# First block's inverse by levels: the product xx of levels 1 to 5 gives way to transposes of XT and a ScalarE copy, in a weave of five more steps a head with 0.94 instead of 1.12 dense steps a round

## The reference

```
decay = jnp.exp(jnp.where(causal, G[..., :, None] - G[..., None, :], -jnp.inf))
kk = jnp.einsum('bhnik,bhnjk->bhnij', k, k)
lmat = jnp.where(strict, beta[..., :, None] * kk * decay, 0.0)
amat = jnp.eye(CHUNK, dtype=q.dtype) + lmat
rhs = jnp.concatenate([v * beta[..., None], k * (beta * jnp.exp(G))[..., None]], -1)
sol = lax.linalg.triangular_solve(amat, rhs, left_side=True, lower=True, unit_diagonal=True)
```

## Time and profile before

| | |
|---|---|
| median of 3 runs | 2263.67 us (2260.33, 2263.67, 2264.84) |
| span of the profiled execution, first to last instruction | 2261.5 us |
| TensorE busy, share of the span | 2066.9 us, 91% |
| DVE, ACT, POOL busy | 42%, 28%, 20% |
| the woven heads and dense tiles | about 116 to 716 us of the span |

### The profile page before, as it was taken

How to read it: one execution, slowest core, us unless ns; L and a number is a source line. 1 busy time by engine, 2 the same in 40 slices (tenths; PEclk the granted TensorE clock), 3 DMA queues, 4 the chain that set the end, 5 groups by cost and what they waited for, 6 DMA issues and landing times.

```text
span 2261.5 us, 24322 instructions
## 1 busy us (share of the span) xinstructions
PE 2066.9 (91%) x10160; PEld 1516.4 (67%) x10160; DVE 943.3 (42%) x1370; ACT 643.6 (28%) x966; POOL 451.9 (20%) x310
## 2 busy tenths in 40 slices
PE   7999999999999979888788879898888899999999
PEld 5878888888887763333333337677655677888787
DVE  7865445433333662111011025865643894222333
ACT  4533422322323311000000024353134763222231
POOL 5432132231322511111111011321001220000021
PEclk9999999999999979998899889999998999999999
DMA  5751421221324369999999964202111133332210
GB/s 168 255 141 47 93 57 38 38 75 45 68 38 152 140 230 397 409 405 406 408 414 406 420 270 169 100 13 72 47 47 37 47 121 122 102 112 75 95 73 38
DMA packets 97657, 361.28 MB, mean 160 GB/s; under 512 B 9850, under 2 KB 34588, under 8 KB 85256
## 3 DMA queue, kind: packets, MB, share of 16 engines
q1 hardware_dynamic: 86800, 335.34, 41.4%
q0 software_dynamic: 8240, 19.00, 2.5%
q10 hardware_dynamic: 2504, 5.35, 0.8%
HBM read 338.94 MB, written 29.10 MB: 163 GB/s over the span
## 4 chain that ended last, share of the span: by engine, by line
PE 81%; DVE 8%; issue 5%; ACT 4%; POOL 1%; DMA 0%; PEld 0%; PEldq 0%; SPq 0%; ACTq 0%; DVEq 0%; POOLq 0%
PE ps L269 77%; PE ps L273 4%; ACT ST L265 1%; DVE H L259 1%; ACT L265 1%; DVE ST L253 1%; DVE BG L253 1%; ACT M L265 1%; DVE sm L2930 0%; DVE WL L253 0%; DVE ML L253 0%; POOL WL L253 0%; ACT M L266 0%; DVE H L256 0%; DVE BG L259 0%
## 5 line engine op out<-in xcount | busy, mean ns | idle before, releaser
L269 PE MATMUL ps<-W,BG 128*64 128x512 f32 x672 | 202.1, 644 | 31.9 <-issue 31.9
L269 PE MATMUL ps<-XH,WS 128*128 128x512 f32 x704 | 218.6, 392 | 0.0
L269 PE MATMUL ps<-HTH,WL 128*128 128x512 f32 x448 | 180.9, 404 | 0.0
L269 PEld LDWEIGHTS ps<-ST 128*128 128x128 f32 x1376 | 167.5, 192 | 8.6 <-POOL ST L253 1.7
L269 PE MATMUL ps<-ST 128*128 128x64 f32 (+1 forms) x1376 | 167.8, 273 | 1.2 <-POOL ST L253 1.0
L269 PEld LDWEIGHTS ps<-XH,WS 128*128 128x128 f32 x704 | 133.4, 189 | 27.8
L2100 DVE COPY BG<-ps 128x512 f32<-128x512 f32 x32 | 22.1, 692 | 293.0 <-PE ps L269 293.0
L269 PEld LDWEIGHTS ps<-W,BG 128*64 128x64 f32 x672 | 62.1, 148 | 120.0 <-issue 118.5
L269 PE MATMUL ps<-XL,WS 128*128 128x512 f32 x352 | 138.1, 392 | 1.8 <-DVE XL L253 1.8
L269 PE MATMUL ps<-M,BG 128*64 128x512 f32 (+1 forms) x336 | 122.7, 552 | 15.7 <-issue 8.4
L263 ACT ACTIVATE BG<-ps 128x512 f32<-128x512 f32 x48 | 28.5, 595 | 377.8 <-PE ps L273 344.2
(11 more groups left out here) (384 smaller groups left out, 4343.2 us busy)
## 6 DMA issues: line engine op xcount, KB each, us to landing
W<-in_w SPq DMA_DIRECT2D x42, 2048.0 KB, 26.3
W<-in_w_in SPq DMA_DIRECT2D x27, 2048.0 KB, 10.3
ST<-in_w SPq DMA_DIRECT2D x14, 2048.0 KB, 25.4
U<-in_w SPq DMA_DIRECT2D x14, 2048.0 KB, 28.0
M<-in_w SPq DMA_DIRECT2D x13, 2048.0 KB, 28.3
HT<-in_w SPq DMA_DIRECT2D x13, 2048.0 KB, 27.9
W<-in_w_ffn_in SPq DMA_DIRECT2D x22, 1024.0 KB, 7.6
ypad<-BG SPq DMA_DIRECT2D x23, 512.0 KB, 15.1
```

The source lines that it names most:

```text
L269: return p.e.matmul(o, lhsT=l, rhs=r, start=start, stop=stop, skip_group_check=True)
```

## The change

At levels 1 to 5, `xx` is no longer the product of `XT` and `Y`. When DVE has updated `XT`, TensorE transposes all of it (`p_turn4`), and ACT copies from the transpose the half of the columns that the next level's `y` reads. `X` after `x0` is likewise copied only in that half. DVE loses the subtraction of `xx`. A level now has three steps, `y`, `xt` and `xx`, so that a head has 33 rounds and the four pairs 132; the rate becomes 0.94. `VB`, which lies in `X`, now waits for the `y` of level 6.

```diff
@@ p_head
             for n in range(1, 7):
                 p.wait_ge(lc_done[h % 2], 6 * (h // 2) + n)
-                if 1 < n < 7:
+                if n > 1:
                     p.wait_ge(*B["xx", h, n - 1].free())
                 p_half(("y", h, n), b0, C, firsts(X, n))
                 yield
                 p.wait_ge(*B["y", h, n].free())
-                if n > 1:
-                    p.wait_ge(*B["xt", h, n - 1].free())
+                p_half(("xt", h, n), b0 + 2, Y, seconds(XT, n))
+                yield
                 if n < 6:
-                    p_half(("xx", h, n), b0 + 1, XT, firsts(Y, n))
-                p_half(("xt", h, n), b0 + 2, Y, seconds(XT, n))
-                yield
+                    p.wait_ge(*B["xt", h, n].free())
+                    p_turn4(("xx", h, n), b0 + 1, XT)
+                    yield
@@ v_head
-                if n < 6:
-                    t = B["xx", h, n]
-                    v.wait_ge(*t.full())
-                    if n == 1:
-                        v.wait_ge(*B["x0", h].free())
-                    else:
-                        v.wait_ge(*B["xx", h, n - 1].free())
-                    tt(v, firsts(X, n), firsts(X, n), packed(t, n), SUB).then_inc(t.drained)
...
-            v.wait_ge(*B["xx", h, 5].free())
+            v.wait_ge(*B["y", h, 6].full())
             tt(v, VB, four(t.at), col4(beta[:, :, h]), MUL).then_inc(t.drained)
@@ s_head
-            act(X, four(t.at), ACT.Copy).then_inc(t.drained)
+            act(firsts(X, 1), firsts(four(t.at), 1), ACT.Copy).then_inc(t.drained)
...
                 act(firsts(Y, n), packed(t, n), ACT.Copy).then_inc(t.drained)
                 yield
                 yield
+                if n < 6:
+                    t = B["xx", h, n]
+                    s.wait_ge(*t.full())
+                    act(firsts(X, n + 1), firsts(four(t.at), n + 1), ACT.Copy).then_inc(t.drained)
+                    yield
@@ heads
-            weave([lambda h=h: one(h) for h in range(8)], 2, back, 1.12)
+            weave([lambda h=h: one(h) for h in range(8)], 2, back, 0.94)
```

## The result

| | before | after |
|---|---|---|
| median of the runs | 2262.03 us (4 runs, 2260.33 to 2264.84) | 2301.93 us (4 runs, 2297.65 to 2307.04) |
| span of the profiled execution | 2261.5 us | 2295.4 us |
| woven stage, first `rb,cst` matmul to first matmul of the merging products | 116.56 to 717.12, 600.56 us | 115.89 to 750.73, 634.84 us |
| TensorE idle in it | 16.0 us | 44.8 us |

What follows compares the result with a forecast made beforehand. TensorE's own instructions were taken to set the woven stage's pace. Terms -19.0 + 1.2 + 3.0 + 0.6 + 0.4 - 0.7 + 0.9 = -13.6 us took the span from 2261.5 to 2247.9, median about 2250; range 2243 to 2258.

Steps and rivals of the forecast that it cites:

- The wait of 0.72 us for POOL's mask at level 2: TensorE's wait for GpSimd's mask in the woven stage was to vanish under a third leg of cover: -0.7 us.
- The longer chain within a level: Three legs per level instead of two; waits at the turns only in two or three levels of the first pair: +0.4 us.
- the one on the third leg: Rival: ACT or DVE come late at the turns in most levels; 0.5 us each leaves 2260 us; chance 0.09.
- The price of transposes: The transposes replacing the product in each level: 104 ns each, 0.84 us for a pair's eight.
- the changes between head and dense steps: TensorE's switches in the woven stage: 119 instead of 106, at 0.09 us each, +1.2 us.
- The bare rounds: Eight rounds without dense work: round 1 costs +3.0 us, rounds 17 and 50 together +0.6, the others 0.
- The turns' leg: Worst leg, xt to turn in the convolution's rounds: TensorE waits 0 to 0.2 us; the rival put 0.5 or 0.7.
- columns set the price: Rival: a transpose costs twice a 64-column instruction, so xx saves 0 instead of 19 us: 2267; chance 0.03.
- The clock: Round 1's new wait may lower TensorE's clock afterwards, losing 0 or 1.7 us; half was put in: +0.9 us.
- the prediction's own signs of being wrong: Turn waits for ST over 5 us, stage clock under 0.97 by over 0.01, or experts' weights arriving when before.
- the clock does not hold through the transposes: Rival: each of twenty turns in the levels drops the clock, 1.7 us each, 34 us added: 2284; chance 0.05.
- The end: After the woven stage, the experts' stage: what the woven stage gains or loses is passed to the end nearly whole.

Runs made afterwards that it cites:

- e1: The changed kernel with GpSimd making the masks of levels 2 to 6 two steps earlier, nothing else changed: 2259.53 us, ratio 0.9994.
- e3: The changed kernel with xx again a TensorE product with DVE's subtraction, in its own step ahead of xt, masks left late: 2310.95 us, ratio 1.0224.
- e5: The changed kernel with xx again a product in its own step, as in e3, and masks two steps early, as in e1: 2282.99 us, ratio 1.0092.
- e4: The changed kernel with a rate of 1.0 instead of 0.94: 2285.44 us, ratio 1.0104.
- e11: The changed kernel, masks where they were, with the count of due dense work starting at 0.07: 2297.88 us, ratio 1.0168.
- e9: e1 with the level-1 mask one step earlier too and the count of due dense work starting at 0.07: 2260.02 us, ratio 0.9997.
- e10: e9 with the last sums of squares one step later and in the other PSUM bank: 2258.70 us, ratio 0.9985.
- e12: The changed kernel, masks where they were, with DVE doing all weight and activation splits of the woven stage: 2255.68 us, ratio 0.9983.

## Why the prediction was wrong

**The step that failed** is "The wait of 0.72 us for POOL's mask at level 2 has a third leg of cover now and goes: -0.7 us". That wait was read as a lone one, and a longer level as more cover. The cover that counts is TensorE's work between the dense tile's end, which releases ACT's and GpSimd's splits, and the next `y`. It doesn't grow with the number of legs: the removed product was nearly half of it. The very wait that was to go, at level 2 of the first pair, became the 3.38 us at 166.25. Beside it stands the same fault in "The longer chain within a level": it followed ACT and DVE, the engines whose work changes, and left out GpSimd, which got only an empty step. The rows were to be had: 5.4 us from tile end to mask, 6.3 us of cover, and 6.3 - 2.7 = 3.6 us left after the change (3.8 in the row above). In place of -0.7 stand +20.8 us of mask waits and 2.3 more named "issue". No rival named GpSimd's queue either; the one on the third leg spoke of ACT and DVE, and against it of a single wait for a mask, where the trace has two (0.72 and 0.25 us).

The change of 34.3 us in the stage, by the runs (rounding leaves 0.1):

| part | us | from |
|---|---|---|
| product to transposes and the longer weave | -15.8 | work, e1 less before |
| mask waits | +20.8 | 21.8 less 1.0 |
| other waits, the 2.3 of the level-1 mask among them | +8.0 | idle +28.8, less the line above |
| work lost with the mask waits | +21.2 | work, after less e1 |

The last line is the clock's, as far as the traces tell: e1 and the change have the same instructions in the stage. Summed over stretches of 4 us, the granted clock puts 97 us of the stage at the lower level in the change and 54 in e1; half of the difference, 22 us, is an estimate of the work lost by it.

- **The price of transposes** was right. Eight start to the next matmul in 0.79 us, 99 ns each, where 0.84 was taken:

```profile
363.15 1.03 PE L273 MATMUL ps<-cst,ST 128*128 128x128 f32 x8
...
363.94 0.48 PE L269 MATMUL ps<-HTL,WHM 128*128 128x512 f32 x1
```

- With the changes between head and dense steps -19.0 + 1.2 = -17.8 was forecast; the work fell by 15.8 from before to e1, the clock's share in it (0.97 to 0.96) included.
- **The bare rounds.** Round 1's wait came out at 3.29 us (3.36 forecast), that behind the turns at 0.27 (0.3):

```profile
121.23 2.04 PE L269 MATMUL ps<-ST,BG 128*128 128x128 f32 x8 [3.29 <-issue]
...
377.14 1.97 PE L269 MATMUL ps<-ST 128*128 128x64 f32 x16 [0.27 <-ACT ST L263]
```

- **The turns' leg** (`xt`, subtraction, turn) never waited in the changed kernel; this rival fell. The rival "columns set the price" fell with the 99 ns. Its 2267 was a span; the median would be 2269.
- **Waits not foreseen.** The dense tile behind the small sums waits 4.04 us for ACT, where the copy of a `y`, two splits of 1.05 us and a table load now stand ahead of the square root of 0.27:

```profile
229.50 0.38 ACT L263 ACTIVATE ST<-ps 128x256 f32<-128x256 f32 x1 [1.25 <-PE ps L269]
229.78 1.05 ACT L263 ACTIVATE WHM<-W 128x1024 fp32r<-128x1024 f32 x1
230.72 1.05 ACT L263 ACTIVATE WV<-W 128x1024 fp32r<-128x1024 f32 x1
...
231.78 1.28 ACT L265 ACT_TABLE_LOAD   x1
...
233.08 0.27 ACT L265 ACTIVATE sm<-ps,cst 128x16 f32<-128x16 f32 x1
...
233.50 0.77 PE L269 MATMUL ps<-HTL,WHM 128*128 128x512 f32 x1 [4.04 <-ACT sm L265]
```

  The new copies are not the cause: e3 and e5, which have none of them, wait the same 4.04 us, and e4 doesn't. It is the places that the weave of 0.94 gives to the steps.
- **The clock** had the right mechanism, a fall behind a wait, and half the price of one fall (0.9 us). The runs show 21.2 us of work beside 21.8 us of mask waits. Of the prediction's own signs of being wrong this one came: 0.92 where 0.96 was the limit. The rival "the clock does not hold through the transposes" came nearest in sign and fell in mechanism. From 360 to 380 us, with turns in it, the clock was 1.00:

```profile
360.00:380.00 20.00, 19.72 (x125) 17.18 (x124) 8.15 (x14) 6.09 (x13) 4.63 (x3) 1.00 0.14 35
```

  The Trainium skill ("TensorE: Matmul & The Clock Gate", PE-mode transpose) lets transposes not count as activity in the way matmuls do; 0.8 us of them at a time, between matmuls, brought no fall here, and no run has a longer stretch of them in the levels.
- **The end.** That the stage's length is passed on whole was right: 34.3 us of the stage, 33.9 of the span.

## What to carry to other kernels

When work leaves the engine that sets the pace, list every semaphore that its next instruction waits on, and follow each back through the queue of the engine that raises it, those the change doesn't touch included: what is ahead of it there, and what that waits for. Compare the time from that release with the work left as cover. A small operation with early inputs belongs ahead of a large late one in an in-order queue; moving it by one place turned +1.8% into about nothing, and the saving of 16 us in TensorE's work then came out as 6.3 in the profiled span (e1 less before), since 9.7 us of new small waits stood against it, and as 2.0 in the medians.

## What the runs showed of the hardware

- **A wait costs up to twice.** 21.8 us of mask waits went with 21.2 us more work for the same instructions (after against e1), 16.6 with 16.1 (e3 against e5). In e11 against e9 it was 15.9 for 24.4. Not every fall of the clock is behind a wait. In the kernel before, no wait stands between 248 and 303 us, and the clock fell behind the small matmuls of 128x1 in step 1 of the second pair:

```profile
276.46 1.05 PE L269 MATMUL ps<-cst,ST 128*128 128x1 f32 x8
```

```profile
280.00:284.00 4.00, 4.00 (x10) 3.13 (x11) 0.13 (x1) 1.49 (x2) 0.00 (x0) 0.50 0.34 129
```

  And removing small waits singly did not pay: e10 idles 6.1 us less than e1 and works 7.2 us more.
- **DVE stood still while GpSimd's split ran**, both instructions with two inputs in SBUF. In the changed kernel, at level 0 of the first pair:

```profile
138.67 2.71 POOL L253 TENSOR_TENSOR WL<-W,WHU 128x1024 fp32r<-128x1024 f32 x1 [7.33 <-ACT WHU L263]
...
139.22 2.71 DVE L253 TENSOR_TENSOR ST<-cst,ST 128x512 f32<-128x512 f32 x1
```

```profile
141.98 0.72 PE L273 MATMUL ps<-cst,ST 128*128 128x128 f32 x4 [2.76 <-DVE ST L253]
```

  With the split on DVE (e12) the same subtraction took its usual time, and `x0` waited 0.74 us:

```profile
139.10 0.69 DVE L253 TENSOR_TENSOR ST<-cst,ST 128x512 f32<-128x512 f32 x1
```

```profile
139.85 0.66 PE L273 MATMUL ps<-cst,ST 128*128 128x128 f32 x4 [0.74 <-DVE ST L253]
```

  DVE's subtraction ended 0.55 us after GpSimd's split. The Trainium skill ("SBUF — State Buffer", Terms) describes a port pair that one of the two holds for a whole instruction while the other blocks fully; this trace agrees, with 2.71 us instead of 0.69. The wait of 2.76 us ahead of `x0` came of it, and not of the transposes: e3 has it too.
